# Hybrid streaming encoder step: the attention gate is transposed into another PSUM bank, and the order of the first three tiles is rewoven

## The reference, cut to what matters

```python
h = rmsnorm(x, norm_g)
aq, ak, av, ag, gq, gk, gv, gg, glr, cv, cgl, cg = jnp.split(h @ w_in, offsets, axis=-1)
q, k = rmsnorm(heads(aq), q_g), rmsnorm(heads(ak), k_g)
y_attn = band_attention(q, k_all, v_all, sinks, q_pos0) * silu(ag)
y_gla = rmsnorm(gla_chunked(gq, gk, gv, log_a, s0), gla_g) * silu(gg)
y_conv = (silu(layernorm(depthwise_conv(cv * sigmoid(cgl)))) @ w_pw + b_pw) * silu(cg)
y = x + concat([y_attn, y_gla, y_conv]) @ w_out
```

## Time and profile before

| | us |
|---|---|
| device time, median of 3 runs | 1002.54 (1002.08 to 1003.2) |
| the profiled execution, whole | 1004.64 |
| its span from first to last instruction | 1002.9 |
| TensorE busy in the span | 929.5 |
| VectorE busy | 790.3 |
| ScalarE busy | 474.3 |
| GpSimd busy | 201.1 |

### The profile page before, as it was taken

How to read it: one execution, slowest core, us unless ns; L and a number is a source line. 1 busy time by engine, 2 the same in 40 slices (tenths; PEclk the granted TensorE clock), 3 DMA queues, 4 the chain that set the end, 5 groups by cost and what they waited for, 6 DMA issues and landing times.

```text
span 1002.9 us, 15973 instructions
## 1 busy us (share of the span) xinstructions
PE 929.5 (93%) x5713; PEld 818.5 (82%) x5713; DVE 790.3 (79%) x1905; ACT 474.3 (47%) x1166; POOL 201.1 (20%) x250
## 2 busy tenths in 40 slices
PE   5759999999999999998997987999999999999987
PEld 4647888888888888886986886998989898998965
DVE  6578878887888787879878668788888887888974
ACT  7366666666666666657634143041422415142311
POOL 0412222222222222220021221020202112120310
PEclk9879999999999999999999788999999999999989
DMA  9323222222223222135332103204021211203021
GB/s 303 123 97 118 106 106 95 106 106 106 106 106 106 105 106 85 65 111 137 104 107 74 44 22 106 84 1 126 1 89 38 75 53 53 75 8 120 1 74 55
DMA packets 57839, 87.79 MB, mean 88 GB/s; under 512 B 10048, under 2 KB 34496, under 8 KB 57760
## 3 DMA queue, kind: packets, MB, share of 16 engines
q1 hardware_dynamic: 57760, 86.77, 26.5%
HBM read 60.21 MB, written 26.60 MB: 87 GB/s over the span
## 4 chain that ended last, share of the span: by engine, by line
PE 65%; DVE 22%; ACT 5%; issue 3%; DMA 2%; POOL 1%; SPq 1%; POOLq 0%; DVEq 0%; ACTq 0%
PE J L1783 17%; PE J L654 16%; PE J L1942 9%; DVE acc L1460 6%; PE J L669 4%; PE J L1927 4%; DVE osum L1395 3%; PE S L1838 3%; DVE osum L1391 2%; DVE qT L1303 2%; ACT olo L1004 2%; DVE wlo L470 1%; PE S L2096 1%; DVE ptlo L1377 1%; PE T L1821 1%
## 5 line engine op out<-in xcount | busy, mean ns | idle before, releaser
L1460 DVE SCALAR_TENSOR_TENSOR acc<-ub,cwh,acc 128x256 f32<-128x256 f32 (+1 forms) x480 | 224.1, 531 | 0.2
L654 PE MATMUL J<-whi,xhi 128*128 128x512 f32 (+1 forms) x408 | 151.1, 370 | 10.5 <-DVE wlo L470 10.5
L1783 PE MATMUL J<-xbh,whi 128*128 128x256 f32 (+1 forms) x512 | 151.8, 296 | 4.5 <-issue 4.5
L1783 PE MATMUL J<-xbl,whi 128*128 128x256 f32 (+1 forms) x512 | 148.0, 289 | 0.0
L1783 PE MATMUL J<-xbh,wlo 128*128 128x256 f32 (+1 forms) x512 | 147.7, 289 | 0.0
L654 PE MATMUL J<-wlo,xhi 128*128 128x512 f32 (+1 forms) x408 | 147.0, 360 | 0.0
L654 PE MATMUL J<-whi,xlo 128*128 128x512 f32 (+1 forms) x408 | 146.9, 360 | 0.0
L1783 PEld LDWEIGHTS J<-xbh,whi 128*128 128x128 f32 x512 | 98.8, 193 | 7.6 <-issue 7.1
L1783 PEld LDWEIGHTS J<-xbl,whi 128*128 128x128 f32 x512 | 98.8, 193 | 0.2
L1783 PEld LDWEIGHTS J<-xbh,wlo 128*128 128x128 f32 x512 | 98.7, 193 | 0.0
L654 PEld LDWEIGHTS J<-whi,xhi 128*128 128x128 f32 x408 | 78.0, 191 | 22.3 <-DVE xlo L612 9.9
(11 more groups left out here) (270 smaller groups left out, 2270.3 us busy)
## 6 DMA issues: line engine op xcount, KB each, us to landing
out<-res SPq DMA_DIRECT2D x60, 256.0 KB, 2.0
x_normed_scratch<-xraw SPq DMA_DIRECT2D x17, 512.0 KB, 2.9
xraw<-xT SPq DMA_DIRECT2D x16, 512.0 KB, 3.5
xtok<-in_x_prompt SPq DMA_DIRECT2D x16, 512.0 KB, 3.6
res<-in_x_prompt SPq DMA_DIRECT2D x16, 512.0 KB, 4.5
xbraw<-x_normed_scratch SPq DMA_DIRECT2D x16, 512.0 KB, 5.1
res<-out SPq DMA_DIRECT2D x14, 512.0 KB, 4.2
wraw<-in_w_in SPq DMA_DIRECT2D x52, 128.0 KB, 2.5
```

The lines of the kernel that those rows point to most:

```text
L654: last = nc.tensor.matmul(bank[:, 0:width], x[x_slot(ps, t)][:, k, :], w, start=(k == 0 and n == 0), stop=(k == KT - 1 and n == 2))
L1460: nc.vector.scalar_tensor_tensor(acc[:, j, 0:frames], src, w, acc[:, j, 0:frames], ALU.mult, ALU.add).then_inc(conv_step, 1)
L1783: last = nc.tensor.matmul(bank[:, 0:w], wt, x[:, k, 0:w], start=(k == 0 and m == 0), stop=(k == KT - 1 and m == 2))
```

## The change

It does two things.

First, the gate transposes write T1 in place of T2. Their wait for VectorE's low halves of the queries goes; they wait for `rb_taken`, the reading of the last row norms out of T1, instead. The wait for the gate's evacuation moves from `pT(1)` to `pX`.

Second, the order of the bodies -2 to 1 is new. TensorE projects the queries of tile 1 ahead of the gate of tile 0, the keys and values of tile 1 behind the first q and k transposes, the gate of tile 1 in halves around the second scores, and the queries of tile 2 in halves around the first `pT` and `pX`; in body 1, keys and values and the gate of tile 2 take those places and `out(0)` stands ahead of `pT(0)`. ScalarE and VectorE split x of tile 1 earlier, do the q and k norms of tile 0 between weight pieces 19 and 20, and split the output weights 24 to 27 ahead of the first attention and 28 to 31 in the middle of it (before: at the end of body 0, and in body 1). GpSimd scales x of tile 0 ahead of its q and k norm. SyncE loads the pieces 24 to 27 right behind the constants and the cached keys and values only in body 0.

```diff
--- before.py
+++ after.py
@@ -164,6 +164,8 @@
...
+    late, early = out.index(("in", 0, 2)), out.index(("in", 1, 0))
+    out[late], out[early] = out[early], out[late]
@@ -406,7 +408,7 @@
...
-        N_CONSTS_A, N_CONSTS_B = 16 * 7, 16
+        N_CONSTS_A, N_CONSTS_B = 16 * 5, 16
@@ -744,13 +746,9 @@
...
-                             (sinks[HD:P, 0:PAIRS], even_odd[1].partition_broadcast(HD)),
-                             (ckv[:, 0, :], io["cache_k"][0, 0].rearrange("w h d -> w (h d)")),
-                             (ckv[:, 1, :], io["cache_v"][0, 0].rearrange("w h d -> w (h d)"))):
+                             (sinks[HD:P, 0:PAIRS], even_odd[1].partition_broadcast(HD))):
                 sp.dma_start(dst, src).then_inc(consts_a, 16)
-
-            for src, dst in ((io["cache_k"], sk_o), (io["cache_v"], sv_o)):
-                sp.dma_start(dst[0, 0, 0:DEC], src[0, 0, DEC:P]).then_inc(windows_stored, 16)
+            load_weights(sp, A, 3 * KT, 3 * KT + STAGES)
@@ -761,6 +759,8 @@
...
+                if t.n == 0:
+                    load_weights(sp, A, 3 * KT + STAGES, len(A.pieces))
@@ -769,7 +769,11 @@
...
-                    load_weights(sp, A, 3 * KT, len(A.pieces))
+                    sp.wait_ge(ident_loaded, 16)
+                    for i, name in enumerate(("cache_k", "cache_v")):
+                        sp.dma_start(ckv[:, i, :], io[name][0, 0].rearrange("w h d -> w (h d)")).then_inc(ident_loaded, 16)
+                    for src, dst in ((io["cache_k"], sk_o), (io["cache_v"], sv_o)):
+                        sp.dma_start(dst[0, 0, 0:DEC], src[0, 0, DEC:P]).then_inc(windows_stored, 16)
@@ -839,7 +843,17 @@
...
+            def qk_rinv(n):
+
+                pool.wait_ge(n_step, 4 * n.n + 2)
+                nc.gpsimd.tensor_tensor(qms[:, :], qss[:, :], eps_h[:, 0:10], ALU.add).then_inc(n_mean, 1)
+                pool.wait_ge(n_mean, n.n + 1)
+                nc.gpsimd.tensor_tensor(qr[:, :], qms[:, :], mhalf[:, 0:10], ALU.pow).then_inc(n_rinv, 1)
+
             def body_a(t):
+                if t.n == -1:
+                    norm_x(B0)
+                    qk_rinv(B0)
                 when(t + 2, norm_rinv)
...
-                if t.n == -1:
-                    norm_x(B0)
+                if n.real() and n.n > 0:
+                    qk_rinv(n)
@@ -941,16 +949,15 @@
...
+                    split_x_hi(B0 + 1)
...
                 if t.n == -1:
                     split_hi(A, KT, 2 * KT)
                     evacuate(B0, 0, raw[:, 0:512], bank_of("in", B0.n, 0)[:, :])
-                    split_hi(A, 2 * KT, 3 * KT)
-                    split_x_hi(B0 + 1)
+                    split_hi(A, 2 * KT, 2 * KT + STAGES)
+                    evacuate(B0, 1, raw[:, 512:768], bank_of("in", B0.n, 1)[:, 0:256])
                     take_rinv(B0)
-                if t.n == 0:
-                    need(act, n_step, 4 * t1.n)
-                    evacuate(t1, 0, raw[:, 0:512], bank_of("in", t1.n, 0)[:, :])
+                    split_hi(A, 2 * KT + STAGES, 3 * KT)
                 if t.real():
@@ -964,12 +971,16 @@
...
+                    if t.n == 0:
+                        take_rinv(t1)
+                        act.wait_ge(n_step, 4)
+                        evacuate(t1, 0, raw[:, 0:512], bank_of("in", t1.n, 0)[:, :])
...
-                    nc.scalar.activation(gth[:, :], T[2][:, :], ACT.Tanh, scale=0.5).then_inc(gate_tanh, 1)
+                    nc.scalar.activation(gth[:, :], T[1][:, :], ACT.Tanh, scale=0.5).then_inc(gate_tanh, 1)
...
-                when(t + 2, norm_square)
+                if t.n == 0:
+                    split_hi(A, 3 * KT + STAGES, len(A.pieces))
+                else:
+                    when(t + 2, norm_square)
+                if t.n == -1:
+                    split_hi(A, 3 * KT, 3 * KT + STAGES)
...
-                if t.n == 1:
-                    split_hi(A, 3 * KT + STAGES, len(A.pieces))
-                if t1.real():
+                if t.n == 0:
+                    norm_square(t + 2)
+                if t1.real() and t1.n > 0:
...
-                when(t + 2, take_rinv)
+                if t.n >= 0:
+                    when(t + 2, take_rinv)
...
-                if t.fixed and t.n == 0:
-                    split_hi(A, 3 * KT, 3 * KT + STAGES)
@@ -1259,6 +1274,17 @@
...
+            def qk_square(t):
+
+                dve.wait_ge(A.taken[1], t.n + 1)
+                if t.n == LAST:
+                    dve.wait_ge(windows_stored, 16 * 4)
+                need(dve, qk_psum, 2 * t.n)
+                nc.vector.tensor_tensor(qkn[:, :], raw[:, 0:640], raw[:, 0:640], ALU.mult).then_inc(n_step, 1)
+                dve.wait_ge(n_step, 4 * t.n + 1)
+                nc.vector.tensor_reduce(qss[:, :], qkn[:, :].rearrange("p (h d) -> p h d", d=HD), AX.X,
+                                        ALU.add).then_inc(n_step, 1)
@@ -1293,8 +1320,11 @@
...
                 if t.fixed and t.n == -1:
-                    split_lo(A, KT, 3 * KT)
+                    split_lo(A, KT, 2 * KT)
                     split_x_lo(B0 + 1)
+                    split_lo(A, 2 * KT, 2 * KT + STAGES)
+                    qk_square(B0)
+                    split_lo(A, 2 * KT + STAGES, 3 * KT)
...
-                    nc.vector.scalar_tensor_tensor(gth[:, :], gth[:, :], 1.0, T[2][:, :], ALU.add,
+                    nc.vector.scalar_tensor_tensor(gth[:, :], gth[:, :], 1.0, T[1][:, :], ALU.add,
...
+                    if t.n == 0:
+                        split_lo(A, 3 * KT + STAGES, len(A.pieces))
...
-                if t.n == 1:
-                    split_lo(A, 3 * KT + STAGES, len(A.pieces))
...
+                if t1.real() and t1.n > 0:
+                    qk_square(t1)
...
+                if t.n == -1:
+                    split_lo(A, 3 * KT, 3 * KT + STAGES)
...
-                if t.fixed and t.n == 0:
-                    split_lo(A, 3 * KT, 3 * KT + STAGES)
@@ -1793,13 +1815,10 @@
...
+                    project(A, B0 + 1, 0, empty_bank("in", 1, 0))
                     project(A, B0, 2, empty_bank("in", B0.n, 2))
-                    pe.wait_ge(rb_taken, 1)
-                    spread_rinv(B0 + 1)
...
                 if t.n == 0:
-                    for c in range(2):
-                        project(A, t1, c, empty_bank("in", t1.n, c))
                     pe.wait_ge(zeros_a, 4)
@@ -1813,20 +1832,23 @@
...
-                if t1.real() and t.n > 0:
+                if t.n in (0, 1):
+                    project(A, t1, 1, empty_bank("in", t1.n, 1))
+                elif t1.real():
                     project(A, t1, 0, empty_bank("in", t1.n, 0), 0)
+                if t.n == 0:
+                    pe.wait_ge(rb_taken, 1)
+                    spread_rinv(t1)
                 if t.real():
-                    pe.wait_ge(qk_lo, 6 * t.n + 2)
+                    pe.wait_ge(rb_taken, min(t.n + 2, TILES))
                     for j in range(4):
-                        last = nc.tensor.transpose(T[2][:, j * P:(j + 1) * P], agraw[:, j * P:(j + 1) * P],
+                        last = nc.tensor.transpose(T[1][:, j * P:(j + 1) * P], agraw[:, j * P:(j + 1) * P],
...
-                if t1.real() and t.n > 0:
+                if t1.real() and t.n > 1:
...
-                if t.n == 0:
-                    project(A, t1, 2, empty_bank("in", t1.n, 2))
@@ -1847,14 +1869,18 @@
...
-                if t1.real() and t.n > 0:
+                if t.n in (0, 1):
+                    project(A, t1, 2, empty_bank("in", t1.n, 2), 0)
+                elif t1.real():
                     project(A, t1, 1, empty_bank("in", t1.n, 1))
                 if t.real():
                     scores(2)
                     scores(3)
...
-                if t1.real() and t.n > 0:
+                if t.n in (0, 1):
+                    project(A, t1, 2, bank_of("in", t1.n, 2), 1)
+                elif t1.real():
                     project(A, t1, 2, empty_bank("in", t1.n, 2))
...
                 def p_wait(u):
...
                 def pT(g):
-                    if g == 1:
-                        pe.wait_ge(gate_ready, t.n + 1)
@@ -1873,7 +1897,7 @@
...
                 def pX():
-                    pe.wait_ge(rb_taken, min(t.n + 2, TILES))
+                    pe.wait_ge(gate_ready, t.n + 1)
@@ -1901,15 +1925,22 @@
                     if t.n > 0 and t.n < TILES:
                         output(A, t + -1, h, empty_bank("outa", t.n - 1, h))
 
+                if t.n == 0:
+                    project(A, t + 2, 0, empty_bank("in", 2, 0), 0)
+                if t.n == 1:
+                    out(0)
                 if t.real():
                     pT(0)
                     pX()
-                out(0)
+                if t.n == 0:
+                    project(A, t + 2, 0, bank_of("in", 2, 0), 1)
+                out(1 if t.n == 1 else 0)
                 if t.real():
                     pv(0)
                     pT(1)
                 when(t + 2, spread_rinv)
-                out(1)
+                if t.n > 1:
```

(1 more changed line is left out.)

16 lines of the change are left out of this document (1 added, 15 removed).

## The result

The changed kernel takes 979.0 us (median of 4 runs, 978.1 to 981.1) against 1002.7 for the kernel before: ratio 0.9773, 95% interval 0.9761 to 0.9785. The profiled execution takes 978.32 as a whole, span 976.5.

What follows compares the result with a forecast made beforehand. TensorE, busy 93%, was taken to bound the kernel with its work plus waits. Gains 16.7 + 0.3 + 9.2 - 1.2 = 25.0 took 1004.64 to 979.6, less 2.1 for the median: 977.5 us; range 971 to 988, chance 0.8.

Steps and rivals of the forecast that it cites:

- the 0.3 of tile 2: Tile 2: scores wait about 0.6 where the gate waited 0.9, a further gain of 0.3 us.
- the 1.2 taken off for a meeting of engines: Tile 0: `qr` on GpSimd holds up VectorE's pieces 20 to 23, gate ends 1.2 us later (bounds 0 to 1.2).
- No wait of the gate transposes in tiles 3 to 15: Settled tiles, sign in the profile after: the gate transposes' 0.71 us wait is gone, period 25.4.
- the margins: Settled tiles: slack before TensorE would wait elsewhere, 0.8 us at the scores and 0.3 at `pv(0)` for `px`.
- The term 13 x 0.71 = 9.2: Settled tiles 3 to 15: each loses the gate transposes' 0.71 us wait, 9.2 us gained (bounds 0 to 9.2).
- The ledger: Opening up to tile 2, step by step: 28.2 us of waits and slow clock become 11.5, gain 16.7; tile 2 near 82.5.
- ScalarE is free at 32.2: Tile 0: ScalarE finishes splitting output weights 24 to 27 at 32.2 us, then does `agraw`, `qT` and `kT`.
- first landing 29.9: Tile 0: first of output weights 24 to 27 lands at 29.9 us, 6.8 after issue; the last by 31.8.
- pieces 28 to 31 delay the exponentials to 41.8: Tile 0: output weights 28 to 31 land by 41 and delay the exponentials by about 2 us, to 41.8.
- the output weights hold ScalarE: Rival, tile 0: late landings put 6 to 9 us back, settled gain stays, 984 to 986 us; chance 0.18.
- 0.95 or more expected from 20 to 82: Opening, sign in the profile after: TensorE's granted clock at least 0.95; 0.5 us was added for slow clock.
- The first three: Whole kernel, rivals: both parts as worked out (0.58), settled wait only moves (0.14), output weights hold ScalarE (0.18); 971 to 987.

Runs made afterwards that it cites:

- e1: Kernel before with only the gate transposes moved to T1, opening as it was: 986.4 us, ratio 0.9839 to before.
- e2: Changed kernel with the gate transposes put back into T2, so only the new opening is left: 990.8 us, ratio 0.9881 to before.
- e6: Changed kernel with SyncE issuing output weights 24 to 27 ahead of the bias and the sinks: 977.6 us, ratio 0.9750 to before.
- e7: Changed kernel with weights 24 to 27 split later, 28 to 31 in idle gaps, and sinks loaded behind 24 to 27: 974.3 us, ratio 0.9727 to before.
- e11: The changed kernel itself, unaltered, timed again in a later comparison: 979.1 us, ratio 0.9765 to before.
- e4: Changed kernel with eight extra wide matmuls filling TensorE's stop ahead of tile 0's gate transposes: 980.3 us, ratio 0.9775 to before.
- e8: Changed kernel with eleven extra wide matmuls filling TensorE's stop ahead of tile 1's scores: 977.6 us, ratio 0.9753 to before.
- e3: Changed kernel with output weights 24 to 27 split where 28 to 31 were, and 28 to 31 at the end of tile 0: 978.6 us, ratio 0.9753.

## Why the prediction was right, and where it wasn't

The time was 1.5 us from the forecast, and part of that is luck: the settled tiles gave 2.3 more than their term, the opening 4.5 less, the 0.3 of tile 2 didn't come, and the 1.2 taken off for a meeting of engines was not due.

**The gate in T1: mechanism right, term too small.** "No wait of the gate transposes in tiles 3 to 15" holds, and so do the margins: the narrowest, 0.3 at `px`, shows as a single wait of 0.3, in tile 15. The term 13 x 0.71 = 9.2 measured 11.5 over the 13 periods. I had costed a stop by its idle row; e1 and e2 give 0.88 to 0.91 each. The way to read it was there: periods by starts, not idle sums.

**The opening: 16.7 forecast, 12.2 measured.** The ledger, followed to tile 1, has it start at 56.9 (45.1, wait 0.9, 2.8, wait 0.8, transposes 1.0, 2.8, `pv(0)` and `pT(1)` 1.1, wait 1.6, `pv(1)` 0.8). It started at 61.28; from there to tile 2 the ledger has 25.6 and the trace 25.7. So all that is missing, 4.4 us, was lost in tile 0, and the step that failed is "ScalarE is free at 32.2" with its "first landing 29.9" and "pieces 28 to 31 delay the exponentials to 41.8". ScalarE was free at 34.8, pieces 28 to 31 were waited for until 44.07 where the ledger had them landed by 41, and the exponentials began at 45.95. These 4.2 us are the delay: the low halves of tile 2's x hang on the same chain, and TensorE took them up at 50.15 where the ledger had 46.0. I had taken the landing from a small load at the same place in the queue; the weights stood behind the sinks, and e6 shows that the order alone makes 2.8 of the 9.1 us. VectorE's product of the gains was held up to 31.62 by the same loads, which put 0.9 in front of the q and k transposes; I had none there. (0.6 more of their lateness was there at the start: the row norm of tile 0 stood at 20.7, not 20.1.) e7 takes both causes away and tile 2 starts at 82.34, where the ledger had 82.5; but e7 has the pieces in another order than the ledger, so this agreement proves little.

The agreement in tile 1, 25.6 against 25.7, is luck too. The waits were 4.1 us (2.6 and 1.5), not 5.7: the 0.6 at `pv(0)` isn't there and the other two are shorter. Slow clock, of which the ledger had none in tile 1, gave 1.2 back: the same code took 24.58 in e11.

**The rival that came in part** is "the output weights hold ScalarE", with 4 us rather than its 6 to 9, and it was hidden in the total by the larger settled gain.

**Meeting of GpSimd and VectorE: 1.2 taken, 0 measured.** VectorE in the kernel after, first the square, then pieces 20 to 23; GpSimd beside them:

```profile
11.75 2.73 DVE L472 SCALAR_TENSOR_TENSOR wlo<-res,gain,whi 128x512 fp32r<-128x512 f32 x4
...
23.08 3.04 DVE L1283 TENSOR_TENSOR qkn<-raw 128x640 f32<-128x640 f32 x1
...
26.89 2.73 DVE L472 SCALAR_TENSOR_TENSOR wlo<-res,gain,whi 128x512 fp32r<-128x512 f32 x4
```

```profile
22.96 2.48 POOL L604 TENSOR_TENSOR xraw<-xraw,rb 128x1024 f32<-128x1024 f32 x1 [7.04 <-ACT rb L598]
27.06 0.65 POOL L849 TENSOR_TENSOR qms<-qss,eps_h 128x10 f32<-128x10 f32 x1 [1.62 <-DVE qss L1285]
27.79 2.34 POOL L851 TENSOR_TENSOR qr<-qms,mhalf 128x10 f32<-128x10 f32 x1
```

The square, 0.82 elsewhere, met `norm_x` and ended 0.7 behind it, as forecast, and TensorE's work hid it. But the four pieces took 2.73 beside `qms` and `qr`, exactly what four such pieces took alone at 11.75 (first row). It was GpSimd that was slower (`qms` 0.65 against 0.21 in tile 1, `qr` 2.34 against 1.97). The Trainium skill (SBUF — State Buffer, section Who interferes with whom) has a VectorE instruction with two SBUF inputs and a GpSimd instruction that reads SBUF lock each other out, for the whole instruction of whoever issues first. The trace agrees for the long instruction; beside the ten-column ones VectorE was not held at all, and GpSimd, whose two began while a piece ran, took 0.4 us more for each.

**The clock: 0.95 or more expected from 20 to 82, 0.92 measured.** TensorE ran at 1.2 GHz from 38.8 to 45.6 and from 69.5 to 72.9. The granted clock is the fourth number:

```profile
38.00:38.50 0.50, 0.00 (x0) 1.00 1.06 434
38.50:39.00 0.50, 0.47 (x3) 0.78 1.02 401
39.00:39.50 0.50, 0.45 (x3) 0.50 1.07 360
```

It fell during the gate transposes, behind the one stop of 1.81 and ahead of that of 0.68. I had priced this at 0.5 because I looked for the pair of longer stops of before, and that reading of the earlier trace rows was wrong: in the kernel before the clock fell at 40.8, behind the stop of 2.33 and ahead of that of 2.01. In tile 0 it cost nothing, for e4 and e8 show that the late chain stood beside it: a wrong reason that didn't hurt the sum. In tile 1 it cost the 1.2 above. The expected 0.9 of wait for tile 2's x isn't there, since the slow clock used it up.

**Tile 2: 0.3 forecast, 0 measured** (26.34 before, 26.36 after).

**The chances.** The first three add up to 0.90, not 0.85; less the tail below 971 that leaves 0.80 to 0.85 for the range.

**The second pass.** From tile 16 to the end of the span all kernels run the same code but for the gate's bank in tile 16, and the thirteen profiled executions took 534.1 (e6) to 537.1 (before) there. That of before is the slowest of them, and 2.7 of the 26.3 us between the two profiled executions is that. The granted clock goes with it in part: 0.96 there before and 0.97 after, but 0.97 in e3 too, which took 536.0. I had set the forecast against the median for this very reason (2.1), and that step held.
